# Expert weights read from memory in runs of 4 KB: row pairs for gate and up, whole rows for down

## The reference, cut to what matters

```
t = rms_norm(h, m_norm[layer])                       # (512, 1024)
combine = top-1 group, then top-2 of its 4 experts   # (512, 16), two entries per token
for e in range(16):
    hdn = silu(t @ w_gate[e]) * (t @ w_up[e])        # w_gate, w_up: (1024, 512)
    y += combine[:, e] * (hdn @ w_down[e])           # w_down: (512, 1024)
h = h + y
```

## Time and profile before

| | |
|---|---|
| median of 3 runs | 1457.77 us (1449.87 to 1467.19) |
| span of the profiled execution | 1450.9 us |
| TensorE busy with matmuls | 1201.6 us, 83% of the span |
| DVE, ACT, GpSimd busy | 818.5, 717.6, 163.2 us |
| mean granted TensorE clock | 0.92 of full speed |
| weight and activation traffic | 283.42 MB, 138206 packets |
| expert stages | from 300 to 640 us (layer 0) and from 1053 to 1414 us (layer 1) |

### The profile page before, as it was taken

How to read it: one execution, slowest core, us unless ns; L and a number is a source line. 1 busy time by engine, 2 the same in 40 slices (tenths; PEclk the granted TensorE clock), 3 DMA queues, 4 the chain that set the end, 5 groups by cost and what they waited for, 6 DMA issues and landing times.

```text
span 1450.9 us, 15116 instructions
## 1 busy us (share of the span) xinstructions
PE 1201.6 (83%) x5557; PEld 891.3 (61%) x5557; DVE 818.5 (56%) x794; ACT 717.6 (49%) x718; POOL 163.2 (11%) x197
## 2 busy tenths in 40 slices
PE   5999979659898898864998889989489888788880
PEld 3888858546566666543887766667356556565660
DVE  3532352668776777745112166632767776767754
ACT  4432332337666666643222357642446665655742
POOL 1100110100100000012000031100102011101004
PEclk9999999869999999996999999999689999989995
DMA  7452013179999999954221100021389988979935
GB/s 230 115 167 87 1 57 118 56 263 340 325 355 323 330 322 333 353 194 166 81 94 59 58 0 1 0 73 58 116 294 349 337 284 309 328 274 343 323 114 185
DMA packets 138206, 283.42 MB, mean 195 GB/s; under 512 B 11704, under 2 KB 11872, under 8 KB 138160
## 3 DMA queue, kind: packets, MB, share of 16 engines
q1 hardware_dynamic: 119424, 239.09, 47.0%
q0 software_dynamic: 11024, 39.07, 8.6%
q10 hardware_dynamic: 7712, 4.63, 1.0%
HBM read 259.96 MB, written 22.81 MB: 195 GB/s over the span
## 4 chain that ended last, share of the span: by engine, by line
PE 49%; issue 19%; DMA 19%; ACT 5%; DVE 4%; POOL 2%; POOLq 0%; ACTq 0%; SPq 0%; DVEq 0%
DMA pad<-normed_rows,token_now 16%; PE ps L1174 12%; PE ps L1175 11%; PE ps L1176 11%; PE ps L1476 3%; PE ps L1461 2%; PE ps L1488 2%; PE ps L1308 2%; ACT pad L563 2%; PE ps L1192 2%; POOL xn L1627 1%; PE ps L1274 1%; ACT w_hi L420 1%; PE ps L1292 1%; DMA raw<-in_a_w_in 1%
## 5 line engine op out<-in xcount | busy, mean ns | idle before, releaser
L756 DVE TENSOR_TENSOR w_lo<-raw,w_hi 128x2048 fp32r<-128x2048 f32 x96 | 221.0, 2302 | 300.9 <-ACT w_hi L420 300.4
L420 ACT CAST w_hi<-raw 128x2048 fp32r<-128x2048 f32 x96 | 183.2, 1909 | 222.6 <-PE ps L1176 214.7
L756 DVE TENSOR_TENSOR xT_lo<-raw,xT_hi 128x2048 fp32r<-128x2048 f32 x64 | 147.0, 2302 | 78.7 <-ACT xT_hi L420 78.6
L1174 PE MATMUL ps<-xT_hi,s_hi 128*96 128x512 f32 (+1 forms) x392 | 164.1, 419 | 3.5 <-DVE s_lo L913 3.5
L1174 PE MATMUL ps<-w_hi,s_hi 128*96 128x512 f32 x384 | 157.3, 410 | 4.9 <-DVE s_lo L901 4.9
L1175 PE MATMUL ps<-xT_lo,s_hi 128*96 128x512 f32 (+1 forms) x392 | 161.0, 411 | 0.0
L1176 PE MATMUL ps<-xT_hi,s_lo 128*96 128x512 f32 (+1 forms) x392 | 160.8, 410 | 0.0
L420 ACT CAST xT_hi<-raw 128x2048 fp32r<-128x2048 f32 x64 | 121.9, 1911 | 71.7 <-PE ps L1176 71.7
L1176 PE MATMUL ps<-w_hi,s_lo 128*96 128x512 f32 x384 | 155.0, 404 | 0.0
L1175 PE MATMUL ps<-w_lo,s_hi 128*96 128x512 f32 x384 | 154.6, 403 | 0.0
L1174 PE MATMUL ps<-w_hi,xT_hi 128*128 128x512 f32 x320 | 124.7, 390 | 3.3 <-DVE xT_lo L802 1.9
(11 more groups left out here) (245 smaller groups left out, 2115.4 us busy)
## 6 DMA issues: line engine op xcount, KB each, us to landing
raw<-in_m_w_up SPq DMA_DIRECT2D x64, 1024.0 KB, 8.6
xn<-in_m_w_gate SPq DMA_DIRECT2D x60, 1024.0 KB, 8.5
raw<-in_m_w_down SPq DMA_DIRECT2D x60, 1024.0 KB, 8.7
raw<-in_a_w_in SPq DMA_DIRECT2D x12, 1024.0 KB, 5.1
output_table<-pad POOLq DMA_DIRECT2D x32, 384.0 KB
raw<-in_w_kv SPq DMA_DIRECT2D x8, 1024.0 KB, 6.6
raw<-in_a_w_out SPq DMA_DIRECT2D x4, 1024.0 KB, 5.2
raw<-in_m_w_gate SPq DMA_DIRECT2D x4, 1024.0 KB, 9.7
```

The lines of the kernel that those rows point to most:

```text
L420: se.copy(hi_slots[split_slot(c)], raw_slots[raw_slot(c)]).then_inc(A["hi_done"], 1)
L756: ve.tensor_tensor(lo_slots[split_slot(c)], raw_slots[raw_slot(c)], hi_slots[split_slot(c)], ALU.subtract).then_inc(V["lo_done"], 1)
L1174: te.matmul(o, a_hi, b_hi, start=start, stop=False)
```

## The change

Three things change together, so that the products stay the same sums:

1. A block of gate or up now holds row pairs: partition p gets rows 2p and 2p+1 of the first 256 rows of the block, and the same of the second 256. A pair is 4 KB without a break.
2. Which row of the matrix meets which partition follows from that, so `x_transposed` takes every second column: columns 0, 2, 4, ... of 256 for one block and 1, 3, 5, ... for the next (`pair_columns`).
3. A block of down is now 256 whole rows of 4 KB, not 512 half rows. `down_block` therefore does two blocks of rows for both halves of the columns: 12 matmuls again, into two PSUM banks in turn, three at a time.

```diff
             if kind == "d":
-                return w[:, half * BN:(half + 1) * BN].rearrange("(k p) n -> p k n", p=P)
-            return w[half * BK * P:(half + 1) * BK * P, :].rearrange("(k p) n -> p k n", p=P)
+                return w[half * 2 * P:(half + 1) * 2 * P, :].rearrange("(k p) n -> p k n", p=P)
+            return w[half * BK * P:(half + 1) * BK * P, :].rearrange("(j p b) n -> p j (b n)", p=P, b=2)
...
-                sp.dma_start(raw_slots[raw_slot(c)].rearrange("p (k n) -> p k n", k=BK),
+                sp.dma_start(raw_slots[raw_slot(c)].rearrange("p (k n) -> p k n", n=src.shape[2]),
                              src).then_inc(raw_loaded[raw_slot(c)], 16)
...
+            def pair_columns(k):
+
+                first = 2 * P * (k // 2) + k % 2
+                return slice(first, first + 2 * P - 1, 2)
+
             def x_transposed(S, i, slot, loads, reuse=True):
...
                         ins = te.transpose(ps[:, 4 + f, CAP * k:CAP * (k + 1)],
-                                           xg[:, slot, P * (4 * f + k):P * (4 * f + k + 1)], ident[0:CAP, 0:CAP])
+                                           xg[:, slot, pair_columns(4 * f + k)], ident[0:CAP, 0:CAP])
...
             def down_block(half, slot, used):
 
-                for kk in range(BK):
-                    wide = slice(BN * kk, BN * (kk + 1))
-                    ins = three(ps[0:CAP, 2 + half, :], ht_hi[:, kk, :], ht_lo[:, kk, :], hi_slots[slot][:, wide],
-                                lo_slots[slot][:, wide], start=kk == 0, stop=kk == BK - 1)
+                for kk in range(2):
+                    k = 2 * half + kk
+                    for n in range(2):
+                        wide = slice(D * kk + BN * n, D * kk + BN * (n + 1))
+                        ins = three(ps[0:CAP, 2 + n, :], ht_hi[:, k, :], ht_lo[:, k, :], hi_slots[slot][:, wide],
+                                    lo_slots[slot][:, wide], start=k == 0, stop=k == BK - 1)
                 ins.then_inc(used, 1)
```

More of the change, by code:

```diff
@@ L613, in tile @@
                             act.wait_ge(W["lo"], 6 * j + b)
-                        act.dma_start(over_raw.rearrange("p (k n) -> p k n", k=BK),
-                                      expert_block(layer, kind, e, half)).then_inc(W["loaded"], 16)
+                        src = expert_block(layer, kind, e, half)
+                        act.dma_start(over_raw.rearrange("p (k n) -> p k n", n=src.shape[2]),
+                                      src).then_inc(W["loaded"], 16)
                         act.wait_ge(W["loaded"], 96 * j + 16 * (b + 1))
```

## The result

The changed kernel takes 1491.6 us (median of 4 runs, 1482.7 to 1504.2) where the one before takes 1456.8 (median of 4). The ratio is 1.0205, 95% interval [1.0151, 1.0259]: about 2% slower. The profiled execution has a span of 1502.5 us, near the slowest of the four runs, against 1450.9 before; so the 51.6 us between the two traces are more than the 30 us (2.05% of 1457) that the runs give, and the traces are used here for where time goes, not for how much.

The account below looks back on a forecast made before the run. The prediction took the per-expert ring, with TensorE waiting for the next expert's gather, as the bound. Only the later gather counted: 1450.9 + 20.8 = 1471.7 us profiled span, 1478 us as a median (1.4% slower); range 1465 to 1500, wide 1432 to 1520.

Parts of the forecast that it names:

- the ring: Chain repeating once per expert: transposes, down, hidden transposes, ACT taking the result out, store, next gather; 22.2 and 21.0 us a turn.
- The weights are not waited for: Expert weight loads: each block needs 0.2 us less engine time, 38 us over 192 blocks, all hidden, so costed at 0.
- 4.6 us are due to the company: Expert gathers: landing takes 4.5 us with no weights moving, about 9.05 beside the stream; the excess was put on the stream.
- The bounds of 147 and 87 us: Gather's whole excess: +147 us if it grows as one weight packet's time, -87 us if it follows the number of packets.
- rival 2: Gather: half the packets stand ahead, so it gets faster; down to 1371 us, 1414 with a quarter gone; chance 0.18.
- rival 3: Gather: delay ahead of it grows with weight packet length; up to 1605 us, 1495 with a quarter of it; chance 0.09.
- The gather beside the longer packets: Gather on the chain: six turns with single weight packets, each 92 ns longer, land it 0.55 us later; at most 1.0 us.
- The delay ahead of the first byte stays: Gather, from issue until its packets move: taken as unchanged by the longer weight packets, though the rows don't explain this delay.
- From a gather to the time: Expert stages: a microsecond of TensorE wait costs 1.35 us, as the clock falls; 28 x 0.55 x 1.35 = 20.8 us.
- Every second column: Stationary loads of the transposes, line 1308: step of two taken as free, 0 us; 36 us if loads took twice as long.
- rival 4: Transposes, line 1308: step of two slows stationary loads, 1.1 us per tile, 1494 us; decided by loads above 200 ns; chance 0.04.
- The turn between queues: DMA engines: skill's rule changes queue after 9 to 17 descriptors, giving 31 to 59 us more; forecast kept single-packet turns instead.

## Why the prediction was right

The direction, the range and, within a factor of one and a half, the size of the loss were right: 1.4% slower forecast, 2.05% measured, 1478 us against 1491.6, range 1432 to 1520. By its own steps:

- *What bounds the kernel.* Right, and now shown: with the gather off the ring the stage loses its wait and the kernel 7.35% (0.9265). The working had 83.0 x 1.35 = 112 us on the ring; the saving measured is 0.0735 x 1469 = 108 us, 1469 being 1360.9 / 0.9265.
- *The weights are not waited for, their cheaper bytes are worth 0.* Right for this kernel. Of the 38 us of engine time 24 show in queue q1 (682 to 658) and none in the time; 14 to 18 us come out once the gather's wait, which hid them, is gone (1360.9 against 1346.9 and 1343.2).
- *With no weights moving 4.5 us, beside the stream 9.05, so 4.6 us are due to the company.* The difference is right, its reading as the company of the weights isn't: the gathers that land after 9.05 us also have a store ahead in their own queue, and without one the first packet came after 1.65 us beside a full stream. The forecast didn't rest on this. The bounds of 147 and 87 us did, and with them rivals 2 and 3 and the width of the range.
- *The gather beside the longer packets, +0.55 us.* Right in mechanism and about right in size. The part of a gather in which its packets move grew by 0.6 us with the packets alone, and the packets alone cost 1.0182, 27 us [18, 35], where the term had 20.8. In the whole change that part grew by about 1.0 us, the upper value of the working. The step "I take one weight packet between each two of the gather" is a little short all the same, and one gather shows where. The queues in 459 to 461.5 of the kernel before show the whole of it (0.39 MB) beside 0.36 MB of weights. In the changed kernel the gather issued at 469.83 needs 5 us for it, with the packets in 473.5 to 476 and then in 476 to 478.5:

```profile
q1 hardware_dynamic: 124, 0.45, 57.1%
q0 software_dynamic: 86, 0.31, 45.6%
...
q1 hardware_dynamic: 173, 0.70, 87.6%
q0 software_dynamic: 24, 0.08, 11.8%
```

  Four fifths of the gather pass in the first 2.5 us, in which the kernel before moved all of one. The last fifth, 0.08 MB, takes another 2.5 us beside 0.70 MB of weights, 173 packets to 24. The turns are not one for one at the end. That some of the 16 engines finish late, and the gather with the last of them, would fit; the trace doesn't name the engine of a packet.
- *The delay ahead of the first byte stays.* Right. Over all 28 gathers it is 4.9 us before and 4.6 after, and still 4.5 with 8 KB. In the gather above the packets of the GpSimd queue move from 473.5 on, 3.7 us after its issue, and in 472.5 to 473.5 the queue has one record and no bytes to speak of:

```profile
q1 hardware_dynamic: 93, 0.38, 99.6%
q0 software_dynamic: 1, 0.00, 0.1%
```

  So rival 3 (the delay grows with the packet) isn't what happens, and of rival 2 (fewer packets make it shorter) at most 0.3 us.
- *From a gather to the time, 1.35.* Not contradicted, and not well tested. 113.1 - 83.0 = 30.1 us more of waiting in the two profiles stand beside 51.6 us more of span, of which 8 to 14 belong to the step: 1.25 to 1.45 us for each. But the kernel with the new down_block alone, with old packets, has 9.6 us more of waiting and 23.2 us more of span than the kernel before, 2.4 for each. A pair of single executions doesn't fix such a price.
- *Every second column, 0.* Wrong: 1.0098 [1.006, 1.0135], 14 us. This was rival 4, put at 36 us with a chance of 0.04. The loads rose by 56 ns at the least and 76 at the median, at full clock, not by the 141 of its price, and the mark it named (loads above 200 ns) is met by the medians over all loads, 218 and 223. The argument "the step stays within 8 bytes" had no row behind it. The cachelines note in the Trainium skill, "SBUF — State Buffer", would have had full rate as well; the loads at 193 ns against 137 say otherwise for the stationary operand, and the measurement decides.
- *down_block, 0.* Not contradicted: 1.0025 [0.9978, 1.0073].
- *The turn between queues.* By the rule in the Trainium skill, "DMA: Bandwidth & Descriptors", with the rows of a gather in one packet, the sum would have been 31 to 59 us. The packets alone cost 27 us [18, 35]. The row's 20.8 and the low end of the rule lie within the same interval, so this doesn't decide between them. By the rule the gather itself would move 0.8 to 1.6 us longer; the 0.6 us with the packets alone lies under that, the 1.0 of the whole change within it.
- *The marks in the profile.* The packets of q1 and its share came as said. The landings rose by 1.4 us in layer 0 and 0.8 in layer 1 (10.0 and 10.3 us) where 0.5 was said, the wait to 113.1 in place of 98, and the granted clock of the two stages fell to 0.89 and 0.91, more than "a little". As the profiled execution is near the slowest of the changed kernel and that of the kernel before near the fastest, a part of these differences is theirs.

What the sum lacked is one term, the step, put at 0 and measured at 14 us. That it still came within 10 us of the 30 us measured is partly luck: packets and step measured apart are 41 us, and why the whole change costs less than that stays open.

## What to carry to other kernels

A transfer that is cheaper per byte is worth nothing while a small transfer beside it is what the ring waits for, and it can cost: look first for the small one, and give it time by issuing it as early as its buffer allows. Here that was one expert earlier, worth 7%, and only behind it did 4 KB runs gain their 1%. Look also at what goes ahead of it in its own queue. When the order of rows in memory is changed, price the reading side too: a step of two in a float32 stationary operand cost 1.0% in its own run, half as much as the whole change, and still 0.3% where nothing waited for the gather.

## What the runs showed of the hardware that was not expected

- A load of a 96 x 128 float32 stationary operand with every second value takes 193 ns at least and 217 at the median, contiguous 137 and 140 ns, at full clock; at half clock both take about 230. In a kernel where TensorE doesn't wait, the eight transposes took 1.08 us in place of 0.82.
- On the ring a gather of 96 rows lands at 10.1, 8.9 to 9.3, 9.7 and 10.6 us (medians) beside streams in packets of 1, 2, 4 and 8 KB. That is no steady function of the length. With the gather issued earlier 1 and 2 KB differ by 0.1 us in the mean.
- The first packet of a gather behind a transfer of its own queue came near 4.3 or near 6.3 us after the issue, with weight packets of every length; with nothing of its queue ahead for 15 us it came after 1.6 to 2.9 us (eight gathers beside a stream in 2 or 4 KB packets).
- The same 239.09 MB took queue q1 756, 682, 657 and 645 us of all engines in these four. Going from 1 to 2 KB gives 10%, and doubling again gives 4% and 2%.
